# The first attention of a fused transformer kernel: maxima and scores ahead of ratio and transposes

## The reference, cut to what matters

```
s = jnp.einsum('bqhmd,bkhmd->bhmqk', qb, kk).astype(jnp.float32) * scale
p = jax.nn.softmax(s, axis=-1)
p = p[:, :, 0] - lam_full * p[:, :, 1]
return jnp.einsum('bhqk,bkhe->bqhe', p.astype(vv.dtype), vv)
```

## Time and profile before

| | |
|---|---|
| median of three runs | 1050.28 us (1049.89 to 1050.72) |
| the profiled execution | 1049.77 us, span 1048.0 us |
| mean granted TensorE clock | 0.998 |
| busy: TensorE matmuls | 1009.3 us, 96% of the span |
| busy: TensorE weight loads | 908.2 us, 87% |
| busy: VectorE | 814.5 us, 78% |
| busy: ScalarE | 522.6 us, 50% |
| DMA | 210.08 MB, mean 200 GB/s |

### The profile page before, as it was taken

One profiled execution on the slowest core, in us unless ns is written; L12 is line 12 of the kernel. 1 busy time (PEld: TensorE's weight loads), 2 busy tenths in 40 slices (PEclk: granted clock), 3 DMA queues, 4 the chain that ended last, 5 costly groups with the idle time before them and its releaser, 6 DMA issues.

```text
span 1048.0 us, 17165 instructions
## 1 busy us (share of the span) xinstructions
PE 1009.3 (96%) x7160; PEld 908.2 (87%) x7160; DVE 814.5 (78%) x1174; ACT 522.6 (50%) x745; POOL 1.9 (0%) x7
## 2 busy tenths in 40 slices
PE   4999999899999999999999999999999999999996
PEld 2689866799989899999999999999987998998685
DVE  3789869869989888999987566679746568896766
ACT  3633248555544345343564443454347565557763
POOL 0000000000000000000000000000000000000000
PEclk9999999999999999999999999999999999999999
DMA  9869550148998886778575656546653053544031
GB/s 360 301 202 333 206 205 1 42 159 282 333 338 301 298 314 225 240 262 281 181 235 196 233 205 217 197 130 197 202 200 131 4 190 120 184 147 163 22 140 41
DMA packets 118732, 210.08 MB, mean 200 GB/s; under 512 B 4266, under 2 KB 82304, under 8 KB 118656
## 3 DMA queue, kind: packets, MB, share of 16 engines
q1 hardware_dynamic: 117764, 206.55, 57.3%
q10 hardware_dynamic: 892, 2.44, 0.6%
HBM read 207.92 MB, written 1.05 MB: 199 GB/s over the span
## 4 chain that ended last, share of the span: by engine, by line
PE 86%; DVE 8%; ACT 2%; DMA 1%; SPq 1%; issue 1%; DVEq 0%; ACTq 0%
PE PS L1757 12%; PE PS L1758 12%; PE PS L1759 12%; PE PS L1892 11%; PE PS L1896 6%; PE PS L1858 4%; PE PS L1877 4%; PE PS L1859 4%; PE PS L1768 3%; PE PS L1915 2%; PE PS L1916 2%; PE PS L1920 2%; DVE low L1069 2%; PE PS L2084 2%; DMA ada_raw<-in_ada_w 1%; PE PS L2049 1%
## 5 line engine op out<-in xcount | busy, mean ns | idle before, releaser
L609 ACT ACTIVATE high<-raw 128x2048 fp32r<-128x2048 f32 (+2 forms) x147 | 274.4, 1869 | 278.8 <-PE PS L1759 100.8
L1069 DVE TENSOR_TENSOR low<-raw,high 128x2048 fp32r<-128x2048 f32 (+2 forms) x147 | 328.0, 2233 | 98.0 <-ACT high L609 97.4
L1892 PE MATMUL PS<-oHL,high 128*128 128x512 f32 x512 | 129.9, 395 | 0.0
L1892 PEld LDWEIGHTS PS<-oHL,high 128*128 128x128 f32 x512 | 91.8, 188 | 18.7 <-issue 1.6
L1757 PE MATMUL PS<-gH,high 128*128 128x256 f32 x352 | 98.7, 280 | 0.0
L1758 PE MATMUL PS<-gL,high 128*128 128x256 f32 x352 | 98.3, 279 | 0.0
L1759 PE MATMUL PS<-gH,low 128*128 128x256 f32 x352 | 98.3, 279 | 0.0
L1858 PE MATMUL PS<-hH,high 128*128 128x258 f32 x384 | 95.7, 285 | 1.0 <-DVE hL L1319 0.5
L1859 PE MATMUL PS<-hL,high 128*128 128x258 f32 x384 | 94.6, 284 | 0.0
L1036 DVE SCALAR_TENSOR_TENSOR ada_acc<-ada_raw,cond,ada_acc 128x1024 f32<-128x1024 f32 x70 | 89.7, 1282 | 4.7 <-DMA ada_raw<-in_ada_w 2.5
L1858 PEld LDWEIGHTS PS<-hH,high 128*128 128x128 f32 x384 | 72.7, 189 | 2.6 <-issue 1.6
(11 more groups left out here) (351 smaller groups left out, 2117.2 us busy)
## 6 DMA issues: line engine op xcount, KB each, us to landing
raw<-in_ffn_w_in SPq DMA_DIRECT2D x44, 1024.0 KB, 5.5
ada_raw<-in_ada_w SPq DMA_DIRECT2D x82, 512.0 KB, 5.8
raw<-in_ffn_w_out SPq DMA_DIRECT2D x22, 1024.0 KB, 5.1
raw<-in_na_w_in SPq DMA_DIRECT2D x16, 1024.0 KB, 5.4
raw<-in_da_wqkv SPq DMA_DIRECT2D x12, 1024.0 KB, 8.8
raw<-in_sc_w_in SPq DMA_DIRECT2D x12, 1024.0 KB, 6.6
raw<-in_ple_w_gate SPq DMA_DIRECT2D x8, 1024.0 KB, 4.9
raw<-in_mla_w_in SPq DMA_DIRECT2D x7, 1024.0 KB, 5.8
```

The source lines that it names most:

```text
L609: nc.scalar.activation(high[s][:, 0:width(u)], raw[s][:, 0:width(u)], ACT.Copy).then_inc(high_ready, 1)
L1069: V_.tensor_tensor(low[s][:, 0:w], raw[s][:, 0:w], high[s][:, 0:w].bitcast(F), ALU.subtract).then_inc(low_dve, 1)
L1892: MM(bank(b + c), high[s][w(j, c)], oHL[:, :, j, :], start=j == 0, stop=False, skip_group_check=True)
```

## The change

In the loop of the first attention VectorE's `da_probs` is cut in two. `da_sums(i + 1)` takes the inverse of the sums and signals a new semaphore. Then comes `da_max(i + 3)`, and then the rest of `da_probs(i + 1)`, which waits for that semaphore. On TensorE the scores of item i + 3 are issued ahead of the transposes of item i. Nothing is computed that was not before.

```diff
+        sums_inverted = sem("sums_inverted")
...
+            def da_sums(i):
+                seen.next(exp_ready)
+                V_.reciprocal(rsum[:, 2 * i:2 * i + 2], esum[:, 2 * i:2 * i + 2]).then_inc(sums_inverted, 1)
+
             def da_probs(i):
-                seen.next(exp_ready)
-                link(V_.reciprocal(rsum[:, 2 * i:2 * i + 2], esum[:, 2 * i:2 * i + 2]))
+                v.wait_ge(sums_inverted, i + 1)
...
             da_max(0)
             split(first["da_v"] + 2 + RING)
+            da_sums(0)
             da_probs(0)
...
                 if i + 1 < 16:
-                    da_probs(i + 1)
+                    da_sums(i + 1)
                 if i + 3 < 16:
                     da_max(i + 3)
+                if i + 1 < 16:
+                    da_probs(i + 1)
...
             for i in range(16):
                 t, h = divmod(i, 8)
+                if i + 3 < 16:
+                    da_scores(i + 3)
                 seen.next(probs_ready)
                 claim(6)
                 transposes(6, [(k * P, P, Pm[i % 2][:, k * P:(k + 1) * P]) for k in range(4)]).then_inc(made_a, 1)
                 owed(probs_copied, 6)
-                if i + 3 < 16:
-                    da_scores(i + 3)
                 seen.next(probs_copied)
```

## The result

The changed kernel takes 1061.01 us (median of 4 runs, 1060.7 to 1061.18) against 1050.09 (4 runs): ratio 1.0104, 95% interval 1.0092 to 1.0116. It is 10.9 us slower; 1061.2 was forecast. The profiled execution took 1061.15 us with a span of 1059.4, 11.4 more than before. All lines of the code shift by one to seven: L716 is now L717, L2084 is L2091, L2049 is L2056, L1768 is L1775, L1259 is L1263.

A forecast was written before the change was run, and what follows sets the result against it. TensorE was taken as the bound, 2.584 us per item against VectorE's 2.561. Twelve items at +0.90 (10.8) plus 0.3 for the loop's start gave 1060.9 from the profiled 1049.77, about 1061.3 in median terms; forecast 1061.2, range 1058.8 to 1063.0.

The forecast's parts named there:

- The bound: In the first attention's passes with scores, TensorE sets the pace at 2.584 us per item, VectorE slightly faster at 2.561.
- Rival 2: VectorE sets the first attention's pace; scores ahead of transposes fill an existing wait: -1.7 us, 1048.6, no change; chance 0.04.
- The term that counts: On TensorE, items 1 to 12 take 3.48 us each against 2.584, +0.90 per item, 10.8 us in all.
- rival 1: In the items with scores only the raw copy is exposed, handovers cost nothing: +9.1 us, 1059.3; chance 0.15.
- The first pass: At the loop's start the value product of item 0 slips from 156.45 by about 0.26 us, not by whole scores.
- Its sum by the trace: Twelve items and the first pass of the first attention together add 10.8 + 0.3 = 11.1 us.
- item 13, which I had put at 2.28: Behind the passes with scores, items 13 to 15 issue none and keep 2.28 us and the same order.
- The 1.2 us of slack that I gave to the path over the maxima: In the loop, scores, maxima, ratio and product finish 1.2 us before the next transposes are due, so VectorE's reordering costs nothing.
- Behind the loop: After the first attention nothing gives the time back; all that follows slides together.
- rival 3: TensorE's clock falls because the stage idles 0.7 of each 3.48 us: +27 us on top, about 1088; chance 0.02.

The follow-up runs named there:

- tensor_only: The kernel before with TensorE's half alone, scores ahead of the transposes, VectorE keeping its order: 1060.87 us, 1.0105 of before.
- values_later: The changed kernel with the value product of item i - 1 behind the transposes of item i, output and square one item later: 1052.65 us, ratio 1.0026.
- before_longer_vector: The kernel before with one more VectorE instruction of about 0.70 us per item from item 1 on, ahead of the product: 1060.81 us, ratio 1.0103.
- Copy_halves: The changed kernel with ScalarE's copy cut into two halves, the value product starting behind the first: 1058.46 us, ratio 1.0082.
- vector_only: The kernel before with VectorE's new order alone, TensorE keeping transposes, scores, value product: 1067.50 us, ratio 1.0172.

## Why the prediction was right

- *The bound.* Read from two rhythms, 2.584 against 2.561, not from busy shares. The runs bear it out: TensorE's order alone makes the loss (tensor_only), and with the copy covered again the item is TensorE's gapless 2.54 (values_later). That VectorE was only 0.02 behind shows in the 3.28 of before_longer_vector. Rival 2, that VectorE sets the pace and S fills an existing wait, fell with the result and with tensor_only. The Trainium skill's rule on weight-load shares (Trainium Kernel Development and Optimization, Best Practices), which is about the distance to the peak, would have pointed at VectorE if taken as a sign of which engine sets the pace. The trace speaks against that use of it here: TensorE's weight-load share was 64% with no gap in its stream.
- *The term that counts.* Forecast 0.90 us per item, measured 3.491 - 2.584 = 0.907; its parts were 1.09, 1.06 and 0.05 for V to S, S to T and the longer T, and the trace has 1.09, 1.06 and 0.66 against 0.60. Copy_halves and values_later show that the exposed copy is what is paid: a shorter copy shortens the item, a covered one brings it back to 2.54. The second attention's rows were a good source for a transition that the stage itself didn't show; rival 1, without handovers, would have been 1.7 us short (1059.3 against 1061.01).
- *The first pass.* V(0) moved from 156.45 to 156.87. Of these 0.42 us, 0.15 are there before the loop (the two maxima of the run-in start at 153.35 in place of 153.20), 0.27 are the pass; 0.26 was forecast.
- *Its sum by the trace.* V(15) starts at 205.69, before at 194.30: 11.39 us = 0.15 + 0.27 + 12 x 0.907 (156.87 to 198.76, 41.89 us; before 156.45 to 187.46, 31.01 us: 10.88) + 0.09. The forecast had 11.1 for this. That the medians lie only 10.9 apart, and the forecast time 0.2 from the measured one, is in part the scatter of single executions, so the last tenths are luck.
- *Wrong in a detail.* The last 0.09 is item 13, which I had put at 2.28 like the ones behind it. V(12) to V(13) took 201.13 - 198.76 = 2.37, before 189.74 - 187.46 = 2.28. Its product ends at 198.98 + 0.75 = 199.73, its transposes start at 199.79: without scores ahead of them VectorE releases them. They come 0.04 late by it, and last 0.66 in place of 0.60. The 1.2 us of slack that I gave to the path over the maxima holds only while scores stand in front of T, and vector_only shows what it is worth without them.
- *Behind the loop.* As forecast everything slides: the output matrix starts 11.39 us later (209.75, before 198.36), the span grew by 11.4, and the SP queue's longest wait from 57.2 to 69.1 us. The clock didn't fall (rival 3).

## What to carry to other kernels

In a loop of several engines ask of each order what runs on the bound engine while another engine works between two of its steps; an independent block belongs there, and moving it ahead of both steps exposes the other engine's time. Here the block takes 1.06 us in either place, but with it gone T to V shrinks only from 1.59 to 1.34. So 1.06 - 0.25 = 0.81 us are lost, and with 0.10 for V to S in place of V to T that makes the 0.91 per item. A block shorter than what it covers should cost its own length; no run here has one. Compare rhythms (start to start over many items) and not busy shares: two engines can both read 97% or more, and only the slower rhythm is the bound. Before using a serial path's slack from one order, check it in the passes where that order ends.

## What the runs showed of the hardware

- Two float32 score matmuls of 64 rows by 512 columns on different halves of the rows take together as long as one alone: 1.06 us for four records (both maps), 1.06 for two (one map). The Trainium skill says that matmuls in different row groups run at the same time (TensorE: Matmul & The Clock Gate, Part 3); this trace agrees. Splitting the pair cost 14.7 us over 13 items, handovers included.
- The same eight value-product records last 1.06 us where their first weight load starts 0.10 ahead of the first matmul, directly behind the transposes (values_later, load at 162.28, matmuls at 162.38), and 1.16 where both start together, behind scores (before, both at 187.46) or behind a wait for the copy (changed kernel, both at 163.85). V to S is 0.99 in the one case and 1.09 in the other.
- The transposes have the same two lengths: 0.60 us with the load 0.11 ahead (before, load 188.34, matmuls 188.45), 0.66 with both at once (changed kernel, 159.02). This is the 0.05 that the prediction took from the second attention.
- The granted clock stayed 1.00 (2.4 GHz) through 38 us in which TensorE was 80% busy with a gap of 0.69 us in each 3.49.
